# Two RMS norms of a transformer block: the input turned unscaled chunk by chunk, the factor 1/rms multiplied in behind the products

## The reference, cut to what matters

```
x = x + gate * (attention_out @ w_out)              # first block, its last product
h = rms_norm(x, attn_norm_g_2)                      # "norm 1"
w, a, g = token_shift(h @ w_in_2[wag columns])      # 288 columns
cq, ckv, kpe = h @ w_in_2[c columns]                # 1088 columns, then norms of their own
r, k, v = token_shift(h @ w_in_2[rkv columns])      # 3 * 1024 columns
x = x + y2 @ w_out_2                                # second block, its mixer's output
h = rms_norm(x, ffn_norm_g_2)                       # "norm 2"
gate = silu(causal_conv3(h @ w_gate) + b)           # 5632 columns
x = x + (gate * (h @ w_up)) @ w_down
out = rms_norm(x, final_norm_g_2)
```

## Time and profile before

| what | value |
|---|---|
| three timed runs, median | 1992.29 us (1988.07 to 1994.86) |
| profiled execution, its own time | 1993.05 us |
| its span | 1991.3 us (1.75 us lie around it) |
| PE busy | 1892.2 us, 95% |
| POOL busy | 1325.3 us, 67% |
| DVE, ACT busy | 906.2 us (46%), 809.2 us (41%) |
| granted TensorE clock, mean | 0.981 of full speed |

### The profile page before, as it was taken

How to read it: one execution, slowest core, us unless ns; L and a number is a source line. 1 busy time by engine, 2 the same in 40 slices (tenths; PEclk the granted TensorE clock), 3 DMA queues, 4 the chain that set the end, 5 groups by cost and what they waited for, 6 DMA issues and landing times.

```text
span 1991.3 us, 32274 instructions
## 1 busy us (share of the span) xinstructions
PE 1892.2 (95%) x12975; PEld 1582.5 (79%) x12975; DVE 906.2 (46%) x1122; ACT 809.2 (41%) x1095; POOL 1325.3 (67%) x683
## 2 busy tenths in 40 slices
PE   5889999999989899998999999999999999999997
PEld 2668878888657798887789877888888888888886
DVE  1004647560351324565644361654455555733223
ACT  3224444444444454333422444434334343433333
POOL 2448878888239489962543496798888888844442
PEclk8899999999999999999999999999999999999999
DMA  9984545555765356543100145455555555555553
GB/s 328 363 306 164 176 168 175 189 187 190 283 223 180 112 163 212 191 147 127 46 25 4 48 167 176 162 190 189 181 181 187 190 190 180 182 196 197 194 190 127
DMA packets 174433, 352.60 MB, mean 177 GB/s; under 512 B 6735, under 2 KB 19421, under 8 KB 171773
## 3 DMA queue, kind: packets, MB, share of 16 engines
q1 hardware_dynamic: 173437, 346.94, 52.4%
q10 hardware_dynamic: 896, 4.20, 0.6%
HBM read 349.02 MB, written 2.10 MB: 176 GB/s over the span
## 4 chain that ended last, share of the span: by engine, by line
PE 59%; POOL 20%; issue 18%; DVE 2%; ACT 1%; POOLq 0%; DVEq 0%; ACTq 0%
PE bank L919 21%; POOL WL L547 19%; PE bank L921 10%; PE bank L873 6%; PE bank L874 6%; PE bank L875 6%; PE bank L1265 5%; PE bank L1185 1%; PE bank L1195 1%; PE bank L1228 1%; PE bank L395 0%; PE bank L1154 0%; POOL HX L840 0%; POOLq L546 0%; POOL arena L814 0%
## 5 line engine op out<-in xcount | busy, mean ns | idle before, releaser
L547 POOL TENSOR_TENSOR WL<-WR,WH 128x1024 fp32r<-128x1024 f32 (+2 forms) x516 | 1229.4, 2393 | 487.1 <-ACT WH L1478 485.6
L1478 ACT ACTIVATE WH<-WR 128x1024 fp32r<-128x1024 f32 (+2 forms) x560 | 577.4, 1037 | 813.3 <-PE bank L875 450.3
L919 PE MATMUL bank<-HX,WH 128*128 128x512 f32 x1840 | 649.6, 398 | 6.9 <-POOL WL L547 5.2
L921 PE MATMUL bank<-HX,WL 128*128 128x256 f32 x1840 | 515.4, 280 | 0.0
L919 PEld LDWEIGHTS bank<-HX,WH 128*128 128x128 f32 x1840 | 345.6, 188 | 92.5 <-issue 5.9
L873 PE MATMUL bank<-WH,HX 128*128 128x512 f32 (+2 forms) x864 | 339.1, 393 | 12.3 <-POOL WL L547 7.3
L921 PEld LDWEIGHTS bank<-HX,WL 128*128 128x128 f32 x1840 | 347.2, 189 | 0.0
L875 PE MATMUL bank<-WH,HX 128*128 128x512 f32 (+2 forms) x864 | 331.5, 384 | 0.0
L874 PE MATMUL bank<-WL,HX 128*128 128x512 f32 (+2 forms) x864 | 331.3, 383 | 0.0
L873 PEld LDWEIGHTS bank<-WH,HX 128*128 128x128 f32 x864 | 163.0, 189 | 50.9 <-issue 14.0
L874 PEld LDWEIGHTS bank<-WL,HX 128*128 128x128 f32 x864 | 163.2, 189 | 31.1 <-issue 1.9
(11 more groups left out here) (295 smaller groups left out, 1957.9 us busy)
## 6 DMA issues: line engine op xcount, KB each, us to landing
WR<-in_w_in SPq DMA_DIRECT2D x96, 1024.0 KB, 5.0
WR<-in_ffn_w_gate SPq DMA_DIRECT2D x44, 1024.0 KB, 5.1
WR<-in_ffn_w_up SPq DMA_DIRECT2D x44, 1024.0 KB, 5.1
WR<-in_ffn_w_down SPq DMA_DIRECT2D x44, 1024.0 KB, 5.1
arena<-in_w_ada SPq DMA_DIRECT2D x64, 512.0 KB, 9.4
WR<-in_w_out SPq DMA_DIRECT2D x32, 1024.0 KB, 5.1
WR<-in_w_ada SPq DMA_DIRECT2D x16, 1024.0 KB, 5.1
WR<-in_w_in SPq DMA_DIRECT2D x12, 768.0 KB, 4.3
```

The costliest lines, as they stand in the source:

```text
L547: eng.tensor_tensor(half(WL, n % NSLOT, *w), half(WR, n % NSLOT, *w), half(WH, nth(n) % 2, *w), ALU.subtract).then_inc(ready, 1)
L919: pe.matmul(bank[:, :].rearrange("p (h n) -> p h n", h=2), wh[:, k, o], HX[:, :, kk, :], start=kk == 0, stop=False, skip_group_check=True)
L921: last = pe.matmul(bank[:, 0:L], wl[:, k, o], HX[:, 0, kk, :], start=False, stop=kk == KT - 1, skip_group_check=True)
L1478: act.activation(half(WH, nth(n) % 2, *w), half(WR, n % NSLOT, *w), ACT.Copy).then_inc(hi_ready, 1)
```

## The change

X is turned without a factor: `turn_x` now uses the identity (a plain transpose) and needs only the X of its chunk, not the norm. The chunks' groups are turned beside the products that follow: six groups in the w_out chunks 1 to 3 (tiles 6 and 10) and before pieces 9 to 14 of w_out_2; the last two, which need the last chunk of X, at tiles 4 and 6 of the next wide chunk. ACT's copies (`take_one`) and DVE's splits (`split_one`) stand between their other work. h goes to new buffers, HX2 and HX3, since HX is still being read. The factor 1/rms is multiplied in afterwards: in the token form by ACT's copy out of the bank (`scale=rstd`), in the feature form by DVE (`by_token`) against a row that PE spreads over the partitions (`row_of`, ones by diag) and DVE copies (`row_to`). The sine moves behind the second c chunk. RAWF, CV, UPS, AH and AL change places with the freed HX. Banks are dealt out anew.

```diff
-        XN2 = at(13696, TT, D)
-        hf2 = at(17792, 2, 2, L)
+        XN2 = at(0, TT, D)
+        hf2 = at(8192, 2, 2, L)
+        HX2 = sb("HX2", 27088 + 13744, 2, KT, L, dt=F32R)
+        rstd_row = at(6912, L)
...
-        RAWF = at(11264, 4, L + 2)
+        RAWF = sb("RAWF", 20480, 4, L + 2)
+        HX3 = sb("HX3", 27088 + 11312, 2, KT, L, dt=F32R)
+        rstd_row3 = at(22576, L)
...
+            def turn_x(g, base, updated):
+                pe.wait_ge(x_updated, updated + 2 * (g // 2 + 1))
+                to_feature(X, g, 4, base)
+            def row_of(bank, q):
+                pe.wait_ge(xn_ready, 2 * (q + 1))
+                for t in range(TT):
+                    last = pe.matmul(BANK[bank][:, t * P:(t + 1) * P], ones, diag[:, t, :], start=True, stop=True)
+                last.then_inc(row_ready, 1)
+            def beside_out(c):
+                if c == 0:
+                    return taken(8, turn_y)
+                def begin(kk):
+                    if kk in (6, 10):
+                        turn_x(2 * (c - 1) + (kk == 10), 16, 0)
+                return begin
...
-                tok_chunk(n_wo + PIECES * c, c % 2, CH, **(dict(begin=taken(8, turn_y)) if c == 0 else {}))
+                tok_chunk(n_wo + PIECES * c, c % 2, CH, begin=beside_out(c))
...
-            pe.wait_ge(xn_ready, 4)
-            turn_x = lambda g: to_feature(X, g, 4, 16, scaled=True)
-            turn_x(0)
-            turn_x(1)
-            wide_chunk(n_wag, 0, 3 * P, begin=taken(16, turn_x))
+            def last_turns(base, updated, ht):
+                def begin(kk):
+                    if kk in (4, 6):
+                        turn_x(6 + (kk == 6), base, updated)
+                    if kk % 2 == 0:
+                        pe.wait_ge(ht_ready, ht + kk // 2 + 1)
+                return begin
+            pe.wait_ge(x_updated, 6)
+            wide_chunk(n_wag, 6, 3 * P, begin=last_turns(16, 0, 16), hx=HX2)
+            row_of(1, 1)
...
             for m in range(8, 4 * PIECES):
+                if m == 12:
+                    pe.wait_ge(x_updated, 8 + 4)
+                if m in (9, 10, 11, 12, 13, 14):
+                    turn_x(m - 9, 35, 8)
                 out2_piece(m)
-            pe.wait_ge(xn_ready, 6)
-            turn_x = lambda g: to_feature(X, g, 4, 35, scaled=True)
-            turn_x(0)
-            turn_x(1)
-            def gate_up(i, **kw):
+            def turns3(kk):
+                last_turns(35, 8, 28)(kk)
+                if kk == 12:
+                    row_of(7, 2)
...
+            gate_up(0, begin=turns3)
...
+            def take_one(hf, g, base, ht, gains):
+                act.wait_ge(xT_ready, base + g + 1)
+                if g >= 2:
+                    act.wait_ge(ht_ready, ht + g - 1)
+                for f in range(2):
+                    act.activation(hf[:, g % 2, f, :], BANK[4 + (base + g) % 2][:, f * L:(f + 1) * L], ACT.Copy,
+                                   scale=gains[2 * g + f]).then_inc(xT_taken, 1)
...
-            for c in range(4):
-                rest_then_next(n_wo + PIECES * c, rest=c > 0)
-                if c >= 1:
-                    squares(c - 1, XN2, 0)
+            rest_then_next(n_wo, rest=False)
+            for c in range(1, 4):
+                n = n_wo + PIECES * c
+                high(n + 2)
+                squares(c - 1, XN2, 0)
+                high(n + 3)
+                take_one(hf2, 2 * c - 2, 16, 16, gains2)
+                high(n + 4)
+                take_one(hf2, 2 * c - 1, 16, 16, gains2)
+                high(n + 5)
+            high(n_wag + 2)
             squares(3, XN2, 0)
...
+            take_one(hf2, 6, 16, 16, gains2)
+            take_one(hf2, 7, 16, 16, gains2)
+            high(n_wag + 3)
             norm_act(1)
-            take_split(hf2, 8, 16, 16, n_wag, [col("attn_norm_g_2", k) for k in range(KT)])
...
-                        ins = act.activation(dst, BANK[4 + 2 * ((1 + j) % 2) + t][:, b0:b1], ACT.Copy)
+                        ins = act.activation(dst, BANK[2 * (2, 1, 2)[j] + t][:, b0:b1], ACT.Copy, scale=rstd[:, t:t + 1])
...
             for m in range(6, 4 * PIECES + 2):
+                if 11 <= m <= 16:
+                    take_one(hf4, m - 11, 35, 28, gains3)
...
+            high(n_gu + 2)
+            squares(3, XJ, 8)
+            take_one(hf4, 6, 35, 28, gains3)
+            take_one(hf4, 7, 35, 28, gains3)
+            high(n_gu + 3)
             norm_act(2)
...
+                if c == 3:
+                    norm_dve(1)
+                for g in (2 * c, 2 * c + 1):
+                    split_one(hf2, g, 16, 0, HX2)
             make_diag(1)
+            def row_to(dst, bank, count):
+                dve.wait_ge(row_ready, count)
+                own.link(dve.tensor_copy(dst, BANK[bank][:, 0:L]))
+                dve.memset(small[:, 511:512], 0.0).then_inc(row_ready_taken, 1)
+            row_to(rstd_row, 1, 1)
...
+            def by_token(v, row):
+                own.link(dve.tensor_tensor(v, v, row.unsqueeze(1).to_broadcast([P, v.shape[1], L]), ALU.mult))
...
+                    by_token(RAW[:, :, 1:L + 1], rstd_row)
                     own.link(dve.tensor_tensor(SH, RAW[:, :, 0:L], RAW[:, :, 1:L + 1], ALU.subtract))
...
+                by_token(RAWF[:, :, 2:L + 2], rstd_row3)
...
+                by_token(UPS, rstd_row3)
```

88 lines of the change are left out of this document (50 added, 38 removed).

## The result

The changed kernel took 1971.49 us (median of four runs, 1968.17 to 1975.57), the kernel before 1993.57 beside it; the ratio is 0.9904, with a 95% interval from 0.9877 to 0.9931. It is 22 us faster, by its interval 14 to 25. The prediction said 1964, range 1952 to 1971: right in sign, 7.5 us under the measured time, which lies 0.5 us outside its range. The profiled execution (1972.74 us, span 1971.0) is 20.3 us shorter than that of before (1993.05, 1991.3).

A forecast was written before the change was run, and what follows sets the result against it. PE, 95% busy, was taken as the bound, with time to gain at the two norms: 16.6 + 12.0 = 28.6 us off 1993.05, all else at 0, gives 1964.5; predicted 1964 us, range 1952 to 1971.

The forecast's parts named there:

- the two holes: PE's stretches behind w_out and w_out_2 shrink from 37.8 and 38.8 us to 18.35 and 24.0, at full clock.
- six turns: Unscaled turns moved into the w_out chunks at each norm, 0.47 us each, 2.8 us added per norm.
- The first multiplication (1.9) fits without moving silu: FFN round: DVE's gate multiplication fits the 2.7 us slack between convolution's end and ACT's silu; cost taken as 0.
- the second stands ahead of the product gate times up: FFN round: DVE's second multiplication delays only a product nobody waits for within the round; cost taken as 0.
- The Trainium skill's rule that I weighed: FFN: DVE and POOL share an SBUF port lock; POOL would lose 2 x 1.22 us a round, still inside 45.2.
- X of chunks finished at least half a chunk earlier: w_out chunks: moved turns read X finished some 10 us before, so PE does not wait for them.
- The angles: DVE's rotary angles, 45 small instructions ahead of the wag chunk's work; the prediction gave them no term.
- the same chain has more time here: Norm 2: copies, splits, root and diag come in time, since tile 12 comes at 17.9 us; no wait.
- C: Rival: new PE waits at tiles 4, 6 or 12, up to 5 us per norm, or rkv's long spacing, 2 us; chance 0.13.
- B: Rival: the FFN's matmul pairs take the short spacing, saving 8 to 9 us more, 1955 us; chance 0.34.
- D: Rival: slower than before, FFN multiplications hold POOL up and PE waits for low halves every round, 2003 us; chance 0.04.

The follow-up runs named there:

- e3: Changed kernel without the up multiplication in the FFN rounds, its factor applied in the last addition to X instead; 1968.0 us, ratio 0.9897.
- e1: Changed kernel without both FFN multiplications by 1/rms (gate and up), a measurement only as the output lacks the factor; 1967.4 us, ratio 0.9898.
- e11: The changed kernel run again unaltered, beside e9 on the same chip; 1970.5 us, ratio 0.9906.
- e9: Changed kernel with e4's and e6's edits, and norm 2's turns of groups 2 and 4 in the middle of pieces 11 and 13; 1972.1 us, ratio 0.9908.
- e6: Changed kernel with DVE's rotary angles placed behind the work on the wag chunk instead of ahead of it; 1973.8 us, ratio 0.9938.
- e5: Changed kernel with norm 2's turns of groups 4 and 5, and ACT's two copies, one piece of w_out_2 later; 1978.9 us, ratio 0.9948.
- e8: Changed kernel with the edits of e4 (which include e3's), e5 and e6 together; 1965.8 us, ratio 0.9907.
- e12: e9 with norm 2's two diagonal matrices made by ACT behind its root instead of by DVE; 1963.6 us, ratio 0.9868.
- e4: e3 with the gate's factor also multiplied inside the PSUM bank, by four instructions of 512 columns, instead of on SBUF; 1968.1 us, ratio 0.9911.
- e7: Changed kernel with one more PE wait, ahead of the first up chunk until its own gate chunk is done; 1973.7 us, ratio 0.9938.

## Why the prediction was wrong

- **What bounds the kernel, and the two holes: right.** 18.2 and 24 us for 18.35 and 24.0, at full clock; six turns cost 2.9 us for 2.8.
- **"The first multiplication (1.9) fits without moving silu; the second stands ahead of the product gate times up, which nobody waits for within the round", taken as 0: the step that failed, in both halves.** I priced a DVE instruction by its own mean and gave its neighbours nothing. The first one's own length was right, 1.9 us in the mean; the second one's, 3.2, was not. Silu moved: the chain grew by 6.7 us (20.9 to 27.6) and ACT waited 4.0 us for it, 2.8 with the first alone (e3), because the multiplications delayed POOL and took the convolution's free places. But most of the time was lost by the second: nobody waits for it within a round, as I said, but DVE came 3.7 us late to the last gate chunk, and the last product begins with a low part that DVE makes behind that chain. The product lost 3.7 us, of them 0.4 with the first multiplication alone (e3) and none with neither (e1). In e11 it lost 2.1 (241.24): in the first trace the clock fell behind the wait (granted 0.57 from 1720.5 to 1724.5, so mostly the lower of its two levels), in e11 it did not (1.00). Rows that I had shown contained the cause: the four convolution instructions of 256 elements took 7.90 us together, while a 1024-element one alone took 1.22. The median of one instruction against its minimum (1.00 and 0.40) would have told it outright. The Trainium skill's rule that I weighed ("SBUF — State Buffer", "SBUF: two separate sides": an exclusive lock, for a whole instruction) was borne out: 0.40 us alone, 2.4 to 2.6 beside POOL, and 0.69 us for an instruction that works in the bank. I used it for what POOL would lose (2.4 us a round), and that came: POOL's 16 halves took 42 us of a round's 45.2, from 39. I did not use it for what each of DVE's instructions would lose.
- **"X of chunks finished at least half a chunk earlier": wrong for norm 2.** In w_out_2's order a chunk ended one piece (5.4 us) ahead of its turn, and the split that stands before its addition took 4.6 us beside POOL. The stretch took 2.6 us more than forecast; 2.1 of them went when the two turns moved into the middle of their pieces (e9).
- **The angles:** not in the sum at all. DVE made them in 5.3 us where POOL stood still, before; now they take 17, tanh comes late, and the c chunks lose 1.7 us, 1.6 of which e6 gives back.
- **Norm 2's chain, "the same chain has more time here": right by luck.** diag came at 1232.7, 1.2 us ahead of row_of; e5 and e9 show how little it takes to lose it.
- **The rivals.** C (a new wait, 1967 to 1976, chance 0.13) gave the right time, with the wrong places: the last turns and tile 12 waited for nothing. Its other half, the long spacing in rkv, came in nine of thirteen traces of the changed kernels, but in neither of the two of this one. B's spacing in the FFN exists (e8, e12), but not in this kernel's two traces. D's mechanism, DVE and POOL in each other's way, is what worked, at 8 us in all (1.7, 2.6 and 3.7) where it needed 28.6.

## What to carry to other kernels

Where DVE and POOL both work on SBUF, count DVE's instructions and not their elements, and price each at one instruction of POOL (2.4 us here) wherever POOL has work queued; look at the minimum and the median of one form, not at its mean. An added instruction of this kind costs its neighbours' free places as well, and a loop can hide it until an end that depends on DVE shows it. Here a factor per token was cheaper in an instruction that reads a bank (e3, e4), and the small matrix on the critical path was ready in time when ACT made it (e12); both keep work away from SBUF's contest between DVE and POOL. Mending one wait can open the next: e5, e8 and e9 each removed one and gained nothing, since diag then came late.

## What the runs showed of the hardware

- Beside a busy POOL a short DVE instruction on SBUF lasts about as long as one of POOL's, whatever its own size: one of 64 elements up to 1.9 us beside POOL's 128x768 halves (1.8 us each; 0.20 in a pause), one of 256 elements 2.4 to 2.6 beside 128x1024 (2.4 each; 0.40 in a pause). Reading a bank, and writing a bank or SBUF, DVE is not slowed (0.68 to 0.69 us for 512).
- Behind a stop of 4.2 us PE ran at the lower clock (0.64 us a pair instead of 0.35) for some microseconds: in e5 the granted clock was 0.66 from 1238 to 1248, so for most of that time the lower of its two levels (1.2 and 2.4 GHz). Behind the 1.8 to 2.0 us stop at the last product the clock fell in the changed kernel's first trace, e5 and e6 (0.57 to 0.66 over the next 4 to 5 us) and not in e7 and e11 (1.00).
- The wide product has two spacings at full clock, 0.346 and 0.353 us a pair. The same wait of 4.2 us stood before one in e8 and before the other in e5.
